# The even stage and the first output stage of a two-layer trunk in one program, with the first loads of the output stage issued during the last projection tile

## What is computed

```python
def even_mixer(...):
    ...
    def merge(s, h):
        return jnp.concatenate([conv_branch(s), mlstm_branch(h, s)], axis=-1) @ w_out
...
h_lat = layer_norm(DEEPNORM_ALPHA * h_lat + g_l * y_lat, ln_g[layer], ln_b[layer])
```

## Time and profile before

| | us |
|---|---|
| median of 3 runs | 3030.64 (3027.17 to 3031.13) |
| the profiled execution | 3030.1 |
| its span | 3028.3 |
| PE busy | 2884.8 (95%) |
| DVE busy | 1531.3 (51%) |
| ACT busy | 1190.3 (39%) |
| mean granted clock of TensorE | 0.978 |

### The profile page before, as it was taken

One profiled execution on the slowest core, in us unless ns is written; L12 is line 12 of the kernel. 1 busy time (PEld: TensorE's weight loads), 2 busy tenths in 40 slices (PEclk: granted clock), 3 DMA queues, 4 the chain that ended last, 5 costly groups with the idle time before them and its releaser, 6 DMA issues. The chain is left out here.

```text
span 3028.3 us, 38367 instructions
## 1 busy us (share of the span) xinstructions
PE 2884.8 (95%) x15527; PEld 2468.4 (82%) x15527; DVE 1531.3 (51%) x2792; ACT 1190.3 (39%) x1980; POOL 249.6 (8%) x291
## 2 busy tenths in 40 slices
PE   6999999999999999979979997999999999999798
PEld 4788888888888888868867886888888888887587
DVE  6536543554355535543333224666666666665444
ACT  5323312331233123332234213666666666665400
POOL 2100000000000000001220000202102022020000
PEclk9899999999999999989989998999999999999899
DMA  6301131113111311153341321001000101000522
GB/s 190 104 23 53 44 109 31 52 44 108 31 52 44 111 31 50 34 211 119 119 146 39 98 91 39 29 25 32 26 25 26 36 18 33 29 22 18 191 84 84
DMA packets 220177, 200.77 MB, mean 66 GB/s; under 512 B 12037, under 2 KB 190613, under 8 KB 220002
## 3 DMA queue, kind: packets, MB, share of 16 engines
q1 hardware_dynamic: 204946, 176.52, 19.0%
q0 software_dynamic: 4656, 16.56, 1.4%
q10 hardware_dynamic: 10400, 5.24, 0.6%
HBM read 157.34 MB, written 40.95 MB: 65 GB/s over the span
## 5 line engine op out<-in xcount | busy, mean ns | idle before, releaser
L40 PE MATMUL e_pj<-e_u_hi,e_w_hi 128*128 128x512 f32 (+1 forms) x864 | 309.5, 358 | 1.0 <-PEq L57 1.0
L40 PE MATMUL e_pj<-e_u_hi,v_w_hi 128*128 128x512 f32 (+1 forms) x864 | 309.1, 358 | 0.0
L41 PE MATMUL e_pj<-e_u_lo,e_w_hi 128*128 128x512 f32 (+1 forms) x864 | 307.5, 356 | 0.0
L42 PE MATMUL e_pj<-e_u_hi,e_w_lo 128*128 128x512 f32 (+1 forms) x864 | 307.3, 356 | 0.0
L41 PE MATMUL e_pj<-e_u_lo,v_w_hi 128*128 128x512 f32 (+1 forms) x864 | 307.0, 355 | 0.0
L42 PE MATMUL e_pj<-e_u_hi,v_w_lo 128*128 128x512 f32 (+1 forms) x864 | 306.8, 355 | 0.0
L1939 ACT CAST t_pt_hi<-t_ring 128x512 fp32r<-128x512 f32 (+1 forms) x384 | 181.5, 519 | 237.0 <-PE t_ring L2123 237.0
L40 PE MATMUL o_y_bank<-o_w_hi,o_m_hi 128*128 128x512 f32 x576 | 228.1, 396 | 32.8 <-DVE o_w_lo L1313 29.0
L2024 DVE TENSOR_TENSOR t_pt_lo<-t_ring,t_pt_hi 128x512 fp32r<-128x512 f32 (+1 forms) x384 | 216.1, 598 | 52.3 <-ACT t_pt_hi L1939 50.8
L41 PE MATMUL o_y_bank<-o_w_lo,o_m_hi 128*128 128x512 f32 x576 | 226.6, 393 | 0.0
L42 PE MATMUL o_y_bank<-o_w_hi,o_m_lo 128*128 128x512 f32 x576 | 226.5, 393 | 0.0
(11 more groups left out here) (398 smaller groups left out, 6387.6 us busy)
## 6 DMA issues: line engine op xcount, KB each, us to landing
e_w_raw<-in_ev_w_in SPq DMA_DIRECT2D x72, 512.0 KB, 4.7
v_mw<-in_mod_w SPq DMA_DIRECT2D x32, 512.0 KB, 3.8
l_w_raw<-in_od_w_in SPq DMA_DIRECT2D x21, 512.0 KB, 4.0
o_m_raw<-mixT SPq DMA_DIRECT2D x20, 512.0 KB, 5.4
o_w_raw<-in_ev_w_out SPq DMA_DIRECT2D x16, 512.0 KB, 9.6
zgT<-l_lat_q POOLq DMA_DIRECT2D x16, 512.0 KB, 3.6
t_zg<-zgT SPq DMA_DIRECT2D x32, 256.0 KB, 2.7
ogT<-t_zg SPq DMA_DIRECT2D x32, 256.0 KB, 2.0
```

The costliest lines, as they stand in the source:

```text
L40: nc.tensor.matmul(out, whi, xhi, start=first, stop=False)
L41: nc.tensor.matmul(out, whi, xlo, start=False, stop=False)
L42: return nc.tensor.matmul(out, wlo, xhi, start=False, stop=last)
```

## The change

- `stage_out` for layer 0 is called inside `stage_even` and appends its streams to the same block. Between the two there is no block end, no clearing of semaphores and no barrier. The output stage's `Space` is opened in the context of `stage_even`, so the end of the merged program closes two of them, one after the other.
- The output buffers have no room of their own in SBUF; they lie over the buffers of `stage_even` that are free by then (`places`): m slots 0 and 1 and w0 to w4 over `q`, `k` and `v`, w5 over `w0`, slot 2 over `w1`, slot 3 over `h_tok`, w6 to w15 over `u_hi` and `u_lo`, the broadcast rows over the gates and `buf`. The three output banks are made of `pj`, `y` and `z`, the transposes use `x` and `e`.
- SP issues m(0,0), w0, m(1,0), w1 to w5 in the last tile (3, 17), once the convolution stores have landed and all steps are done (`x_done`). w6 and w7 come after the last four stores, and after a wait for all stores m(0,1), m(1,1), w8 to w15.
- In the last tile ACT and DVE split m(0,0), w0 and m(1,0) behind the evacuation of j = 0, and w1 behind that of j = 1 (`EARLY`). The splits of the rest follow after the even stage's work.
- PE waits for the last projection bank to be evacuated and for the second group of `ht_used` before `first_pair`, and for the sixth group before tile 2. POOL waits for the stores and the gate rows before its broadcasts.
- Layer 1's output stage has the same order of work; its buffers are now placed by address.

```diff
@@ stage_even, sync stream
+                if (h, t) == tiles[-1]:
+                    sp.wait_ge(mix_out, 32 * store_at[(h, "conv1")])
+                    sp.wait_ge(x_done, len(steps))
+                    out.load_m(sp, 0, 0)
+                    out.load_w(sp, 0)
+                    out.load_m(sp, 1, 0)
+                    for k in range(1, 6):
+                        out.load_w(sp, k)
                 if t == NTILE - 1:
                     for j in range(2):
                         store(h, j, KD + 2 * h + j, (ht_used, ht_at[(h, j, 2)]))
-            sp.wait_ge(mix_out, 32 * len(stores))
-            sp.wait_ge(g_out, 16 * len(row_at))
@@ stage_even, scalar stream (the vector stream has out.low in the same place)
+        EARLY = {0: [("m", 0, 0), ("w", 0), ("m", 1, 0)], 1: [("w", 1)]}
...
+                    if (h, t) == tiles[-1]:
+                        for part in EARLY.get(j, ()):
+                            out.high(act, *part)
@@ stage_even, end
+        stage_out(nc, a, keep, 0, out, block, {"mix": (mix_out, 32 * len(stores)), "gates": (g_out, 16 * len(row_at)),
+                                               "projected": (pj_free_d, dve_free[(*last_tile, 2)]),
+                                               "y_bank": (ht_used, ht_at[(HEADS - 1, 0, 1)]), "turned": (ht_used, ht_at[(HEADS - 1, 1, 2)])})
@@ stage_out
+        if layer == 0:
+            REST = weights(2, 8) + [("m", 0, 1), ("m", 1, 1)] + weights(8, KM)
+        else:
+            REST = [("m", 0, 0), ("w", 0), ("m", 1, 0)] + weights(1, 6) + [("m", 0, 1), ("m", 1, 1)] + weights(6, KM)
+        REST += [("m", 2, 0), ("m", 2, 1)]
...
+            if layer == 0:
+                for k in range(6, 8):
+                    out.load_w(sp, k)
+                sp.wait_ge(*tail["mix"])
+            else:
...
             load_m(0, 1)
             load_m(1, 1)
-            for k in range(6, KM):
-                load_w(k)
+            for k in range(6 if layer else 8, KM):
+                out.load_w(sp, k)
...
+            if layer == 0:
+                pool.wait_ge(*tail["mix"])
+                pool.wait_ge(*tail["gates"])
...
+            if layer == 0:
+                pe.wait_ge(*tail["projected"])
+                pe.wait_ge(*tail["y_bank"])
             first_pair()
+            if layer == 0:
+                pe.wait_ge(*tail["turned"])
@@ build
-        stage_out(nc, a, keep, 0)
```

More of the change, by code:

```diff
@@ L974, in _ @@
                         after_state(h, n, 0)
+                    if (h, t) == tiles[-1]:
+                        for part in EARLY.get(j, ()):
+                            out.low(dve, *part)
                 if KIND[t] == "conv_x":
@@ L1125, in stage_out @@
+def stage_out(nc, a, keep, layer, out=None, block=None, tail=None):
     ident, mod_col = keep["ident"], keep["mod_col"]
@@ L1131, in stage_out @@
     u_dst = a["u1T"].rearrange("(k p) t -> p k t", p=P)
-    w_src = a["ev_w_out" if layer == 0 else "od_w_out"].rearrange("a (k p) n -> k p (a n)", p=P)
-    first_row = NC if layer == 0 else 0
     half_at = numbered((n, h) for n in range(count) for h in range(2))
[L1135 to L1138, removed]
+    H, YB = OUT_HALF, 3
@@ L1160, in stage_out @@
[L1160 to L1165, removed]
+        if layer == 1:
+            s = Space(nc, ctx, "o1")
+            at = s.nc.sbuf_base + 511 - (s.nc.sbuf_base + 127) % 512
+            names = ["res0", "res1", "y0", "y1", "g_bc", "ln_g", "ln_b"]
+            places = {n: at + 20 * 8 * D + 4 * D * m for m, n in enumerate(names)}
+            places.update(w=[at + 8 * D * k for k in range(KM)], m=[at + 8 * D * (KM + b) for b in range(OUT_SLOTS)], small=at + 20 * 8 * D + 4 * D * len(names))
+            banks = [s.bank(f"y_bank{i}", 2) for i in range(YB)]
+            out = Output(nc, a, s, 1, places, [[b[:, 512 * o:512 * o + 512] for o in range(2)] for b in banks], [s.bank(f"t_bank{g}")[:, :] for g in range(2)])
@@ L1174, in stage_out @@
         u_stored = [s.sem(f"u_stored{b}") for b in range(2)]
-        block = ctx.enter_context(nc.Block())
+        if layer == 1:
+            block = ctx.enter_context(nc.Block())
         cols = lambda o: slice(512 * o, 512 * o + 512)
+        weights = lambda lo, hi: [("w", k) for k in range(lo, hi)]
+        if layer == 0:
+            REST = weights(2, 8) + [("m", 0, 1), ("m", 1, 1)] + weights(8, KM)
+        else:
+            REST = [("m", 0, 0), ("w", 0), ("m", 1, 0)] + weights(1, 6) + [("m", 0, 1), ("m", 1, 1)] + weights(6, KM)
+        REST += [("m", 2, 0), ("m", 2, 1)]
         @block.sync
@@ L1281, in modulate @@
                 act.dma_start(u_dst[:, :, n * P:n * P + P], u_out[b][:, :, :]).then_inc(u_stored[b], 16)
[L1283 to L1293, removed]
+            for part in REST:
+                out.high(act, *part)
             for n in range(count):
                 if n + 3 < count:
-                    split(n + 3, 0)
-                    split(n + 3, 1)
+                    out.high(act, "m", n + 3, 0)
+                    out.high(act, "m", n + 3, 1)
                 if layer == 0:
@@ L1342, in norm @@
                     nc.vector.scalar_tensor_tensor(y[b][:, :], y[b][:, :], rstd[:, :], ln_b[:, :], ALU.mult, ALU.add).then_inc(ln_ok, 1)
-            split(0, 0)
-            split_w(0)
-            split(1, 0)
-            for k in range(1, 6):
-                split_w(k)
-            split(0, 1)
-            split(1, 1)
-            for k in range(6, KM):
-                split_w(k)
-            split(2, 0)
-            split(2, 1)
+            for part in REST:
+                out.low(dve, *part)
             if layer == 0:
```

138 lines of the change are left out of this document (88 added, 50 removed).

## The result

The changed kernel took 3012.4 us (median of 4 runs, 3006.3 to 3015.1) against 3030.9 for the kernel before beside it (4 runs, 3027.2 to 3034.6): ratio 0.9935, interval 0.9924 to 0.9947. That is 18.5 us less; the forecast was 19.8.

A forecast was written before the change was run, and what follows sets the result against it. PE, busy 95% of the span, bounds the kernel; only its waits and low clock can be won. 20.86 - 0.2 - 0.9 = 19.8 us less gives 3011.0 us, with 8 in 10 for 3007.5 to 3016.5.

The forecast's parts named there:

- The seam, 20.86 us: Between even and output stage: PE loses 16.34 us idle and 4.52 us to low clock and the m(1,0) wait.
- The landing of m(1,0): In the last tile: m(1,0) arrives 7.2 us (early bound, taken) or 11.6 us (late bound) after the first load's issue.
- free point: Before the even stage's last transposes: latest m(1,0) landing that costs PE nothing, put at 1287.5.
- rivals 1 and 4: Before the even stage's last transposes: m(1,0) late, 3016, chance 0.15; or so late the kernel is slower, 3035, chance 0.03.
- rival 1: Before the even stage's last transposes: m(1,0) lands late, costing 2.4 us plus 2.7 of clock; 3016, chance 0.15.
- The ninth row, 0.2: At k = 8 of `first_pair`: PE stalls 0.2 us for m(0,1), m(1,1) and w8.
- the late bound: At k = 8 of `first_pair`: m(1,1) there at 1312.9 and w8 at 1314.3, a stall of 0.6 us.
- Rival 2: At k = 8 of `first_pair`: broadcasts delay the second eight rows, a stall of 5.0 us; 3015.6, chance 0.10.
- The second clearing, 0.9: At the output stage's end: a second semaphore clearing and barrier add 0.9 us to the path.
- The later stages: Behind the merged program: work only shifted in time, though clock steps may differ; width of the case 3007.5 to 3013.5.
- Rival 3: In the last tile: SP reaches the loads only behind the last stores; gain some 6 us, 3025, chance 0.03.

The follow-up runs named there:

- the repeat: The changed kernel run once more with nothing changed, beside the kernel before: 3012.7 us, ratio 0.9934.
- The runs with dummies: The kernel before, plus 40 or 72 unused identity transposes ahead of the first output stage's first product: 3031.9 us with 40, 3033.9 us with 72.

## Why the prediction was right, point by point

**The seam, 20.86 us: confirmed.** Up to tile 2 it gave 20.81 in the profile of after, and A is shorter by 20.83 in the repeat, where nothing else intervenes; 16.34 of idle time and 4.52 of low clock had been read from the earlier trace rows. By the kernels in between, in this order, it splits into 5.9 for the merge (the kernel with late loads), 7.6 for the loads in the last tile (247.37 - 239.81) and 7.4 for the splits there. That the low clock would go too was right, because both of its causes went, the wait for w0 and that for m(1,0). The runs with dummies show that the first alone is not enough.

**The landing of m(1,0).** Between the bounds of 7.2 and 11.6 us, at 8.0, and so before the free point. The reason given, that the broadcasts no longer share the engines, is the one that fits the three landings: 11.6 us with the broadcasts 0.4 us behind the first load, 9.8 with them 3.2 us behind it (late loads), and 8.0 without them. They were not varied alone. The experiment with m(1,0) last moved it to 13.9 and confirmed the chain of waits behind rivals 1 and 4 and its free point to 0.5 us. The price of the clock in rival 1 was 2.7; the runs show 1.4 (wait of 5.1), 2.9 (3.4), 2.8 (4.6) and 2.5 (12.5), so it is not a function of the wait's length.

**The ninth row, 0.2.** It was zero, with 1.1 us to spare. With the 1.6 us of this execution taken off, m(1,1) came 0.7 us ahead of the late bound and w8 at least as much. m(0,1) landed 7.8 us after its issue (1302.35 to 1310.14), not 12.0, so the 12.0 us were indeed too late a bound for it. Rival 2 failed by its own counterargument, that those 12.0 us already hold a full queue. Three broadcasts more were needed to bring its stall, and then it cost more than rival 2 said: it had left out the clock, 2.9 us on top of 3.4.

**The second clearing, 0.9: right, but the end grew by 1.3.** The clearing is 0.9 (0.7 to 1.6 from the first DRAIN on). The term was mis-sized by what lies before it: B grew by 1.31, and the 0.4 between are in the time from the landing of POOL's last store to the DRAIN, which the prediction took as unchanged.

**The later stages.** "Only shifted" held within their scatter. From the next stage's first load to the end of the span, the thirteen profiles, all of kernels whose instructions from there on are the same, took 1469.0 to 1472.7 us; the profile of before had 1469.57, the one of after 1470.81. The sum of the terms is 20.83 - 1.31 = 19.5 without the low stretch in tile 2 and 17.9 with it; the medians' difference of 18.5 lies between, and the scatter of the rest is wider than what separates them.

**Rival 3** (loads only behind the stores) would have been 3025, a gain of some 6 us; the kernel built so shortens A by 5.9 and took 3027.7, a gain of 3.0. The end takes 1.3 back, and the rest is within the scatter.

## What to carry to other kernels

A seam between two stages costs PE its wait and the slow stretch behind it. Moving the next stage's first loads into the last tile only pays in full if their preparation is placed there too, ahead of the old stage's last work by no more than that work has slack; here, added in this order, the merge gave 5.9, the early loads 7.6 and the place of the splits 7.4 of 20.8 us. Before filling an idle engine to keep its clock, look at what is late behind the first operand: here it was the second one, and the filler was worth nothing. After merging, look at the end of the merged program too: what was taken away at the seam (here 1.3 us of it) may come back there.

## What the runs showed of the hardware that was not expected

- Behind the same two short waits of PE (1.31 and 0.68 us) the granted clock fell for 3.4 us in one execution and not in another of the same program, and in four of ten profiles in all. Nor did a wait's length set the price: behind a wait of 5.1 us it was 1.4, behind one of 3.4 it was 2.9.
- The clock came up during 72 transposes on 128 columns and fell again behind a wait of 2.55 us, in which the share of the DMA engines was 1.04.
- The clearing of a range of semaphores grows with what it holds: 287 and 391 ns for the two sets, 651 for both in one.
- A load of 512 KB landed 8.0 us after its group's first issue as third, and 13.9 as eighth. The Trainium skill ("DMA: Bandwidth & Descriptors", Anatomy of one DMA) fits one transfer issued from GpSimd as 2.0 us plus its bytes at 436 GB/s; these loads are issued by SP. As an estimate from that page, three loads in a row, 1.57 MB, would be there after 5.6 us. The measured 8.0 is longer, and decides.
